# Gated memory: mixers' sums of squares as rows, their factors spread by products of 40 rows

## What is computed

```python
o = o.transpose(0, 2, 1, 3).reshape(B, T, A_HEADS, 2 * A_DIM)
o = rmsnorm(o, subln_g) * (1.0 - lambda_init)             # 4 heads of 128 channels
...
o = hgrn2_chunkwise(q, logf, k, v).transpose(0, 2, 1, 3)
o = rmsnorm(o, norm_g) * jax.nn.silu(g_pre.astype(f32)).reshape(B, T, H_HEADS, H_DV)   # 4 heads of 64
...
mix = jnp.concatenate([y_m, y_a, y_h], axis=-1).astype(x.dtype)
x = x + jnp.einsum('bte,ed->btd', mix, w_out[l])
```

## Time and profile before

| what | value |
|---|---|
| median of 3 runs | 3433.91 us (3433.42 to 3436.01) |
| the profiled execution: time, span of its instructions | 3434.2 us, 3432.2 us |
| PE busy, share of the span | 3375.6 us, 98% |
| DVE, ACT, POOL busy | 1413.6, 1030.5, 1510.6 us |
| mean granted clock of PE | 0.993 of full |

### The profile page before, as it was taken

One profiled execution on the slowest core, in us unless ns is written; L12 is line 12 of the kernel. 1 busy time (PEld: TensorE's weight loads), 2 busy tenths in 40 slices (PEclk: granted clock), 3 DMA queues, 4 the chain that ended last, 5 costly groups with the idle time before them and its releaser, 6 DMA issues.

```text
span 3432.2 us, 41693 instructions
## 1 busy us (share of the span) xinstructions
PE 3375.6 (98%) x16634; PEld 2733.5 (80%) x16634; DVE 1413.6 (41%) x2641; ACT 1030.5 (30%) x1298; POOL 1510.6 (44%) x522
## 2 busy tenths in 40 slices
PE   8999999999999999999999999999999999999999
PEld 7878878688888888885887887967888878778887
DVE  6565377554353523235211127854101168541010
ACT  2222333631213222224322234343212244432121
POOL 4545552045455545540454554502646545026453
PEclk9999999999999999999999999999999999999999
DMA  7444322034443433230223222201222222012222
GB/s 285 179 152 192 103 89 72 18 153 150 164 165 140 180 140 132 88 97 18 86 84 106 87 94 77 81 13 62 94 92 97 98 74 74 26 49 98 98 98 74
DMA packets 58747, 358.63 MB, mean 104 GB/s; under 512 B 10208, under 2 KB 10592, under 8 KB 21856
## 3 DMA queue, kind: packets, MB, share of 16 engines
q1 hardware_dynamic: 58592, 356.50, 29.0%
HBM read 354.38 MB, written 2.10 MB: 104 GB/s over the span
## 4 chain that ended last, share of the span: by engine, by line
PE 93%; DVE 5%; issue 1%; ACT 1%; DMA 1%; SPq 0%; POOL 0%; DVEq 0%; ACTq 0%
PE LP L594 84%; PE XB L594 8%; DMA big<-w_ada 1%; PE LP L971 0%; PE XB L818 0%; DVE XB L2121 0%; PE XB L854 0%; DVE big L2517 0%; DVE big L2301 0%; ACT E L1368 0%; DVE XB L2793 0%; DVE E L2527 0%; DVE big L2303 0%; DVE S L2480 0%; DVE rt L2561 0%
## 5 line engine op out<-in xcount | busy, mean ns | idle before, releaser
L1891 POOL TENSOR_TENSOR w_lo<-ring,w_hi 128x2048 fp32r<-128x2048 f32 (+3 forms) x274 | 1127.3, 4114 | 636.3 <-ACT w_hi L1368 636.1
L594 PE MATMUL LP<-u_hi,w_hi 128*128 128x512 f32 x2424 | 950.8, 392 | 2.6 <-ACT u_hi L1368 2.4
L594 PE MATMUL LP<-u_hi,w_lo 128*128 128x512 f32 x2440 | 952.2, 390 | 0.0
L594 PE MATMUL LP<-u_lo,w_hi 128*128 128x512 f32 x2424 | 926.2, 391 | 0.0
L594 PE MATMUL LP<-big_r,w_hi 128*128 128x512 f32 x2520 | 781.5, 391 | 5.8 <-POOL w_lo L1891 3.3
L1368 ACT ACTIVATE w_hi<-ring 128x2048 fp32r<-128x2048 f32 (+3 forms) x274 | 471.7, 1721 | 672.4 <-PE LP L594 669.4
L594 PE MATMUL LP<-big_r,w_lo 128*128 128x512 f32 x1508 | 588.1, 390 | 0.0
L594 PEld LDWEIGHTS LP<-big_r,w_hi 128*128 128x128 f32 x2520 | 473.5, 188 | 106.9 <-DVE h L2371 4.2
L594 PEld LDWEIGHTS LP<-u_hi,w_hi 128*128 128x128 f32 x2424 | 456.7, 188 | 111.7 <-issue 16.7
L594 PEld LDWEIGHTS LP<-u_hi,w_lo 128*128 128x128 f32 x2440 | 459.8, 188 | 95.8
L594 PEld LDWEIGHTS LP<-u_lo,w_hi 128*128 128x128 f32 x2424 | 457.8, 189 | 94.6
(11 more groups left out here) (372 smaller groups left out, 3490.7 us busy)
## 6 DMA issues: line engine op xcount, KB each, us to landing
ada_in<-w_ada SPq DMA_DIRECT2D x66, 1024.0 KB, 4.9
ring<-w_in SPq DMA_DIRECT2D x20, 1024.0 KB, 4.8
ring<-w_gu00a SPq DMA_DIRECT2D x11, 1024.0 KB, 7.1
ring<-w_gu00b SPq DMA_DIRECT2D x11, 1024.0 KB, 6.6
ring<-w_gu01a SPq DMA_DIRECT2D x11, 1024.0 KB, 6.7
ring<-w_gu01b SPq DMA_DIRECT2D x11, 1024.0 KB, 6.7
ring<-w_gu10a SPq DMA_DIRECT2D x11, 1024.0 KB, 6.7
ring<-w_gu10b SPq DMA_DIRECT2D x11, 1024.0 KB, 5.1
```

Of the source, the lines that this page charges most:

```text
L594: return pe.matmul(o, lhsT=lhsT, rhs=rhs, start=start, stop=stop)
L1891: gp.tensor_tensor(used_part(q, w_lo[:, slab % RING, 0:width]), used_part(q, ring[:, slab % RING, 0:width]), used_part(q, w_high(q, width) ...
```

## The change

The sums become rows: a selector of 44 columns, `selh`, mostly zeros, with two columns of ones (32 apart), is the stationary operand (40 columns of it, shifted for each head), and the 512 squared columns move. All six products accumulate in rows of one bank; every sum stands twice, in rows i and 32 + i. ACT takes the root of 40 rows by 512, DVE the reciprocal of them; then DVE rounds the 40 rows and subtracts in rows 32 to 39, so that one product of 40 rows with rounded operands spreads a factor and its rest. Six such products take the place of 48 with float32 operands. The order changes too: `weighted(0)` comes first, sums stand between the first steps, the spreads come one step later, the last two behind the first two output chunks, and DVE's `quarter_rest` of the second slab moves behind all of `mix_scale`.

```diff
+        selh = cst2[:, NCONST2 + 2 * T + 78:NCONST2 + 2 * T + 122]
+        def head_sums(i):
+            return selh[:, 3 - i:43 - i] if i < DIFF_H else half_sums(i - 2, 40)
+        mix_rows, mix_parts = big[0:40, GI, :], big_r[0:40, GF, :]
+        def mix_bank(i):
+            return LP[0][:, 0, :] if i == 5 else XB[3][:, :]
...
                 def mix_sum(i, square):
-                    for b in range(NB):
-                        o = 8 * b + i
-                        if i < DIFF_H:
-                            last = mm(XB[3][:, o:o + 1], square[:, blk(b)], cc("ones", 0, 1))
-                        else:
-                            last = mm(XB[3][:, o:o + 2], square[:, blk(b)], selw[:, 6:8])
-                    return last
+                    return mm(XB[3][0:40, :], head_sums(i), square, start=i == 4, stop=i == 3)
...
                 def mix_spread(i):
                     if i == 0:
                         pl.got("mix_recip")
-                    else:
+                    elif i < 5:
                         pe.wait_ge(s("mix_scaled"), 6 * l + i)
-                    for b in range(NB):
-                        if i < DIFF_H:
-                            last = mm(XB[3][:, blk(b)], mix_col(i, b).to_broadcast([P, P]), cc("ident"))
-                        for j in range(2) if i >= DIFF_H else ():
-                            last = mm(XB[3][half(j), blk(b)], mix_col(2 * i - 4 + j, b).to_broadcast([P, 64]), cc("ident"))
-                    last.then_inc(s("mix_spread"), 1)
+                    one = sel40[0:40, 64 * i:64 * i + 1].to_broadcast([40, P]) if i < DIFF_H else halves_of(i - 2)
+                    mm(mix_bank(i), one, mix_parts).then_inc(s("mix_spread"), 1)
+                weighted(0)
+                pe.wait_ge(s("o_taken"), pl.head)
+                memory_scores(1)
                 pl.got("mix_squared", 4)
...
-                out_products(0, range(2, 5))
+                out_products(0, range(2, 4))
+                mix_spread(4)
+                mix_spread(5)
+                out_products(0, range(4, 5))
                 pl.got("den_copied")
...
                 link(ts(selw, cc("blk64", 0, 32), 0.0, None, ALU.mult))
+                link(ts(selh, cc("blk64", 0, 44), 0.0, None, ALU.mult))
+                for r in (0, 32):
+                    link(dve.tensor_copy(selh[:, 3 + r:4 + r], cc("ones", 0, 1)))
...
+                def mix_factors():
+                    low = slice(32, 40)
+                    pl.got("mix_root")
+                    link(dve.reciprocal(XB[3][0:40, :], mix_rows))
+                    link(ts(mix_parts, XB[3][0:40, :], 1.0, None, ALU.mult))
+                    tt(mix_parts[low, :], XB[3][low, :], mix_parts[low, :].bitcast(F32), ALU.subtract)\
+                        .then_inc(s("mix_recip"), 1)
...
-                    quarter_rest(pl.cut + (n - 1) // 4, (n - 1) % 4)
-                    if n == 3:
-                        pl.got("mix_root")
-                        dve.reciprocal(mix_col(0), mix_col(0)).then_inc(s("mix_recip"), 1)
-                    if n >= 4:
-                        mix_scale(n - 4)
+                    if n <= 4:
+                        quarter_rest(pl.cut, n - 1)
+                    if n == 4:
+                        mix_factors()
+                    if n >= 5:
+                        mix_scale(n - 5)
...
                 for c in (5, 6, 7):
                     rest_mixed(f"wo{l}", c)
+                for i in range(4):
+                    quarter_rest(pl.cut + 1, i)
                 dve.wait_ge(s("den_cols"), l + 1)
```

More of the change, by code:

```diff
@@ L1277, in mix_spread @@
                         pl.got("mix_recip")
-                    else:
+                    elif i < 5:
                         pe.wait_ge(s("mix_scaled"), 6 * l + i)
-                    for b in range(NB):
-                        if i < DIFF_H:
-                            last = mm(XB[3][:, blk(b)], mix_col(i, b).to_broadcast([P, P]), cc("ident"))
-                        for j in range(2) if i >= DIFF_H else ():
-                            last = mm(XB[3][half(j), blk(b)], mix_col(2 * i - 4 + j, b).to_broadcast([P, 64]), cc("ident"))
-                    last.then_inc(s("mix_spread"), 1)
+                    one = sel40[0:40, 64 * i:64 * i + 1].to_broadcast([40, P]) if i < DIFF_H else halves_of(i - 2)
[3 more added lines that the diff above has]
+                memory_scores(1)
                 pl.got("mix_squared", 4)
                 for cp in range(2):
-                    mix_sum(4 + 2 * cp, tabs[:, cp, :])
-                for hh in range(3):
+                    mix_sum(4 + cp, tabs[:, cp, :])
+                mix_sum(0, wk[:, 0, :])
+                memory_scores(2)
+                for hh in (1, 2):
                     mix_sum(hh, wk[:, hh, :])
-                pe.wait_ge(s("o_taken"), pl.head)
-                memory_scores(1)
-                weighted(0)
+                weighted(1)
                 pl.got("mix_squared")
                 mix_sum(3, tabs[:, 2, :]).then_inc(s("mix_summed"), 1)
-                for n in range(2, 2 * NB + 1):
+                for n in range(3, 2 * NB + 1):
                     if n < 2 * NB:
@@ L1300, in _ @@
                     weighted(n - 1)
[L1301 to L1303 removed]
+                    if n >= 5:
+                        mix_spread(n - 5)
                 src = mixed(f"wo{l}")
@@ L1340, in _ @@
                 last.then_inc(s("num_summed"), 1)
+                pe.wait_ge(s("mix_scaled"), 6 * (l + 1))
                 out_products(1, range(2, 6))
@@ L1844, in _ @@
                     high_quarter(pl.cut + (n - 1) // 4, (n - 1) % 4)
-                    if n == 2:
+                    if n == 3:
                         pl.got("mix_summed")
[L1847 to L1850, removed]
+                        f(mix_rows, XB[3][0:40, :], ACT.Sqrt, scale=1.0 / P, bias=cc("eps")[0:40, :])\
+                            .then_inc(s("mix_root"), 1)
+                    if n >= 6:
+                        act.wait_ge(s("mix_scaled"), 6 * l + n - 5)
+                        high_mixed(f"wo{l}", n - 4)
                 high_quarter(pl.cut + 1, 3)
-                act.wait_ge(s("mix_scaled"), 6 * l + 4)
-                high_mixed(f"wo{l}", 5)
+                for c in (4, 5):
+                    act.wait_ge(s("mix_scaled"), 6 * l + c - 1)
+                    high_mixed(f"wo{l}", c)
                 for i in (4, 5):
@@ L2992, in _ @@
                         memory_weights(n)
-                    quarter_rest(pl.cut + (n - 1) // 4, (n - 1) % 4)
-                    if n == 3:
-                        pl.got("mix_root")
-                        dve.reciprocal(mix_col(0), mix_col(0)).then_inc(s("mix_recip"), 1)
-                    if n >= 4:
-                        mix_scale(n - 4)
-                    if n >= 6:
-                        rest_mixed(f"wo{l}", n - 4)
-                mix_scale(5)
+                    if n <= 4:
+                        quarter_rest(pl.cut, n - 1)
+                    if n == 4:
+                        mix_factors()
+                    if n >= 5:
+                        mix_scale(n - 5)
+                    if n >= 7:
+                        rest_mixed(f"wo{l}", n - 5)
+                rest_mixed(f"wo{l}", 4)
+                for i in (4, 5):
+                    mix_scale(i)
                 for c in (5, 6, 7):
                     rest_mixed(f"wo{l}", c)
+                for i in range(4):
+                    quarter_rest(pl.cut + 1, i)
                 dve.wait_ge(s("den_cols"), l + 1)
```

2 lines of the change are left out of this document (1 added, 1 removed).

## The result

The changed kernel takes 3441.07 us (median of 20 runs, 3438.92 to 3442.33) and the kernel before, on the same chip, 3435.26 (20 runs, 3432.83 to 3436.98). The ratio is 1.0018 with a 95% interval of 1.0011 to 1.0024: 5.8 us longer. The time is 5.4 us above the forecast of 3435.7, near the upper end of the range. The profiled execution took 3441.81 us, with a span of 3440.0; that of the kernel before took 3434.2, so the two profiles differ by 2 us more than the medians do.

The account below looks back on a forecast made before the run. PE, busy 98% of the span, was taken to bound the kernel. Stage -3.4, constants +1.2 and clock behind new waits +4.0 gave +1.8 on the profiled 3434.2, or 3436.0; median 0.3 lower, 3435.7 us, range 3430.5 to 3441.5.

Parts of the forecast that it names:

- no difference: Whole kernel: a change below 0.2% (6.9 us) counts as none; chance of "same" 0.83.
- Full clock: Changed stage, clock kept: -0.9 us in the first layer, -2.5 in the second, -3.4 together.
- Sums: Twelve row sums take 5.3 us against 5.4 a layer; keeping the clock up gains 1.6 and 3.2 us.
- rival 4: The 40-column sums don't keep the clock, so 1.6 and 3.2 us are not won: 3440.5 us; chance 0.07.
- Waits: New PE waits in each layer: 2.8 to 2.9 us for DVE's factors, 2.7 for ACT's denominators ahead of the transposes.
- Rival 3: Factors not late, the 512-column reciprocal taking 0.7 us: 3426.4 us with the clock kept at the transposes; chance 0.05.
- Constants: Making the new selector on DVE, its 44-column instruction waiting for POOL: +1.2 us, PE's wait there from 3.3 to 4.5.
- Clock behind the waits: Half clock behind two in three of four new PE waits: 2.7 losses x 1.5 us = +4.0.
- rival 2: Half-clock stretches behind the four waits add up to more than 18 us, making the kernel slower, 3442.6 us; chance 0.11.

Follow-up runs that it names:

- e2: Changed kernel with 6 idle products (twelve instructions, results unused) on PE ahead of the first spread, where it waits for the factors: 3430.39 us.
- e10: Changed kernel with DVE's reciprocal of 40 rows taken over 256 of its 512 columns, output not the reference's: 3433.39 us.
- e9: Changed kernel with four surplus products (eight instructions, 128 rows by 256 columns) behind the spread that waits for the factors: 3439.55 us.
- e7: Kernel before with an unread reciprocal of 40 rows by 512 columns and two conversions put into DVE's step 4: 3441.86 us.
- e3: Changed kernel with the factors made on ACT as exp(-0.5 ln(mean + eps)) and no reciprocal on DVE: 3425.75 us.
- e6: Changed kernel with spreads 4 and 5 behind one chunk of output products in place of two: 3436.88 us.
- e5: Changed kernel with one zeroing of 122 columns in place of the three of 32, 44 and 46 in the constants: 3439.80 us.

## Why the forecast came out 5.4 us low

That no difference was forecast held by 1.1 us, and in part by luck: a term of the sum was off by more than twice.

**Full clock: right, to 0.9 us.** e2 has the changed kernel's timetable with a full clock up to the transposes. Its stages hold 3.4 us of half clock behind the transposes each, worth 1.5 us by the changed kernel's own two layers (56.60 without, 58.07 with). So at full clock the changed stage takes 52.7 and 52.6 us. Against before that is -0.4 and -2.1, -2.5 in all; the forecast had -0.9, -2.5 and -3.4.

**Sums: right.** The four rows's form took the same 1.91, and the clock was 1.00 up to 2324; rival 4 is out.

**Waits: right in place and nearly in size.** For the factors 2.81 (2.8 to 2.9 forecast), for the denominators 2.28 (2.7), for POOL's `w_lo` 4.5 (4.5). Rival 3 is out by the 3.35 us of the reciprocal.

**Constants: right for the wait.** The rule in the Trainium skill (SBUF — State Buffer, Who interferes with whom), that DVE and GpSimd share one port pair under an exclusive lock, agrees with the trace: 3.15 us for 44 columns with POOL at work, 0.19 without. PE's wait there grew by 1.2; the first mark of the stage moved by 0.8, since the clock ahead of it differs too: a stretch of 3.4 us at half clock at 1484 us is gone, and behind the wait at the constants it is 6.8 us long in place of 3.4. The forecast had no term for the clock there.

**Clock behind the waits: the term that failed.** The forecast counted 2.7 losses among four waits at 1.5 us, +4.0. Against e2's full-clock stage the changed kernel lost 3.9 us a layer to the 10.2 us behind the factors, and 1.5 once behind the transposes: 9.3. Together -2.5 + 9.3 + 0.8 = 7.6 of the 7.8 us of the profiled spans; the medians differ by 5.8. The number of losses was right, three of four, and so was the price of a short one, 1.5. What was wrong is the length behind the factors, taken from waits for L2803 and L2932 of similar length, behind which 3.3 us at half clock was usual: it was 10.2, and cost 3.9 in place of 1.5. This is the mechanism of rival 2, with two long stretches and not four. Its condition, more than 18 us at half clock, was met (10.2 + 10.2 + 3.4 = 23.8); only the result that it gave, a time above the 0.2%, was not reached.

Its cause was also put too simply. The forecast went by the length of a wait. The runs show that it does not decide: behind 1.21 us of waiting the clock was half for 10.2 us (e10), behind 2.81 with surplus products after it for 0 and 3.4 (e9), behind 2.23 with spreads of 128 rows after it for 0 and 3.4 (e7), and without a wait not at all with the same 40-row spreads (e3). So in these runs the long stretch came only where both stood together: a wait, and behind it the narrow remains of the memory and spreads of 40 rows. The forecast noted the short products behind this wait in rival 2 and did not charge for them. The rule of the Trainium skill (TensorE: Matmul & The Clock Gate, Why this matters for your kernels) goes by the length of idle gaps, and by it none of these waits would cost the clock; the trace does not agree, at 2.81 us (changed kernel) and least of all at 1.21 (e10). Which of the two, spreads or remains, keeps the clock low was not separated (e7 has the same remains, with other spreads, but its wait is shorter and comes a step later), nor why the transposes' wait of 2.28 us was followed by half clock in some layers and not in others.

**Where the gain of the change went.** Without the reciprocal (e3) the changed kernel is 8.9 us faster than before. The reciprocal of 512 columns between steps 4 and 5 costs some 15 us: by the medians 10.7 from the changed kernel to e2, where the clock holds, and 4.6 from e2 to e3, where the wait is gone too. By the traces the stages give 6.3 and 6.9. Of the first step 1.8 us lie between the layers, where nothing ties them to the reciprocal, and e2 loses 1.5 more than the changed kernel behind the transposes. With that loss taken out, the clock behind the factors costs 7.8 (3.9 a layer, as above) and the waits 6.9: about half each. e7 supports it from the other side, by 1.7 to 7.9 us for the same work put into the kernel before.

## What to carry to other kernels

Turning sums from columns into rows relieves PE (at full clock the stages here are 0.4 and 2.1 us shorter) and lengthens DVE's part: a reciprocal of 32 columns becomes one of 512, and an engine that is 41% busy over the span is late at one place. Price a new wait of PE together with the clock behind it, read from a place where the same kind of products follow: here two waits of 2.8 us cost some 15, about half of it in clock. Before a small DVE instruction is moved out of POOL's way, look at which one comes next.

## What the runs showed of the hardware that I had not expected

The granted clock stayed at half for 10.2 us behind a wait of only 1.21 us (e10), and for 13.7 and 17.1 us where two more 40-row spreads stood among the first output products (e6; but for 13.7 without them, too, in the second layer of e5), although PE was busy throughout (10.20 of 10.20 us in the changed kernel's first window at half clock). Six products (twelve instructions) whose result nobody reads made the kernel 10.7 us faster by the medians (e2). DVE's wait for POOL hit instructions of 2, 8, 44 and 46 columns alike (2.35, 3.13, 3.15 and 2.59 us), while those of one column ran beside POOL in 0.15.
